# mLSTM gate rows stacked over 128 partitions in a two-layer hybrid trunk on one core

## The chip, the cores and the metric

The kernel runs on one core of one Trainium2 chip. What counts is its time on the device in microseconds (us), here the median of three runs. One further execution was recorded by the hardware profiler; all rows below are from that one.

## What is computed

Two layers of a block over 256 latent tokens with a prefix of 256 context tokens, width 1024. Each layer projects the normed tokens into the inputs of three branches (a bidirectional chunkwise mLSTM, grouped attention, a short convolution), merges them through gates, and ends with a squared-relu MLP. The change touches the mLSTM gates: an input gate i and a forget gate f for 2 directions and 4 heads, 16 numbers per token. Cut to that part:

```python
gates = (mg.reshape(bsz, n, 2, 2, M_HEADS) + gate_b).transpose(0, 2, 3, 4, 1)   # direction, i or f, head, token
for direction in range(2):
    rev = (lambda t: jnp.flip(t, axis=2)) if direction == 1 else (lambda t: t)
    ctx_state, h_c = run(q_c, k_c, v_c, g_c, init)        # log_i = g[:, direction, 0], log_f = log_sigmoid(g[:, direction, 1])
    _, h_l = run(q_l, k_l, v_l, g_l, ctx_state)
    outs.append((rev(h_l), rev(h_c)))
# in the scan, for each token t and each earlier token s:
#   w = exp(F_t - F_s + i_s - m_t),  F = running sum of log_f,  m = running maximum
#   h_t = sum_s (q_t . k_s) w v_s / max(|sum_s (q_t . k_s) w|, exp(-m_t))
```

The kernel does it for all 512 tokens at once, from rows per gate: F (running sum of log f), a = i - F, M (running maximum of a) and e = exp(-F - M).

## The kernel before

The tokens (512 columns: 256 context, 256 latent) stay transposed in SBUF, the model width over the partitions. All large products are done in a high and a low part (hH, hL, wH, wL), three products each, in panels of 256 output columns: SyncE loads a panel into raw, ScalarE writes its high part (L1428), VectorE the rest (L1845), TensorE runs the 48 products of it (run_panel). One list, PLAN, written by make_plan, sets the order of all steps, and each engine walks it in that order. Small steps lie between the panels. Four PSUM banks (pc) are shared by all small steps; `use(st, name, bank)` gives each step its bank and its turn on it, and TensorE claims a bank by waiting until the engine that read it before has freed it.

The steps that matter, in the order of PLAN, in each layer:

- gate_w: ScalarE and GpSimd write high and low part of the gate weights into wg, columns 0 to 15 and 32 to 47; the rest of wg is zero. GpSimd does its part after a few memsets, among them ones_row and M_parts.
- panels mk 0 and mk 1, then gate_tok (L1262, L1263): TensorE writes the gate rows to bank 1, 128 partitions of which 0 to 15 and 32 to 47 hold something. VectorE copies 48 partitions into g_rows and writes them reversed in time (context and latent each by itself) into g_back (L2103 to L2108).
- panel mq 0, then gate_sel (L1271, L1272): with the constant table sel, TensorE picks 8 rows (4 heads of either direction) for i into bank 2 and for f into bank 3, each from g_rows plus g_back: four products.
- gate_exp, gate_scan, gate_e, gate_e2 beside panels mq 1 and mv 0 to 2: VectorE and ScalarE make F_run, a_run, M_run, e_run (8 rows of 512 tokens) and their reversed forms a_back, M_back, e_back.
- gate_cols (L1280): TensorE turns the four row tiles a_run, a_back, e_run, e_back, each in four pieces of 128 tokens, so that tokens lie on partitions: 16 products with a corner of the identity. VectorE copies the 128 columns to g_col (L2156).
- weigh, weigh_late and value for each head. weigh spreads M over the partitions (m0, m1; L1293) and makes the scores of the first keys (s0, s1; L1300); weigh_late those of the last keys (s2; L1308). ScalarE and VectorE make the weights EP from them, GpSimd masks them (L1806), value (L1324) multiplies with v, into banks 0 to 3 in the order of its results, and VectorE evicts these (L2188 to L2199). In layer 1 only latent queries are computed: m0 and m1 share one bank, s0 and s1 another, and weigh, weigh_late follow value of the head before directly; then come norm_h, a panel mo, turn (banks 2 and 3; L1334) and the head's own value.

Of the kernel before, what the change touches and what calls it, by code (L numbers as in the profile page):

```python
# [20 lines left out]
F32 = mybir.dt.float32  # L21
F32R = mybir.dt.float32r
ALU = mybir.AluOpType
# [41 lines left out]
def make_constants():  # L65
# [32 lines left out]
    return np.concatenate([ident, row_sum, rot, np.cos(ang), np.sin(ang), sel.reshape(P, 32), one_row, pair_row],  # L98
# [6 lines left out]
CONST_COLS = FIRST_COLS + P + LAT + LAT + 32 + 8 + 8  # L105
# [76 lines left out]
def make_plan():  # L182
# [270 lines left out]
    for st in plan:  # L453
# [100 lines left out]
def trunk(nc, x, c, ctx_in, c_ctx, w_ada, b_ada, norm1, norm2, w_in, gate_b, mnorm, qnorm, knorm, conv_w,  # L554
          w_pm, w_pa, w_pc, w_out, w_up, w_down, fnorm, consts, out):
    ctx = ExitStack()
    with ctx:
# [18 lines left out]
        names = ["g_rows", "g_back", "f_pre", "f_neg", "f_exp", "log_f", "F_run", "a_run", "e_run"]  # L576
        rows = {n: at(n, [16, TOK], F32, Y + i * TOK * 4) for i, n in enumerate(names)}
        rows["a_back"] = at("a_back", [16, TOK], F32, Y + 9 * TOK * 4)
        rows["e_back"] = at("e_back", [16, TOK], F32, Y + 10 * TOK * 4)
# [5 lines left out]
        for n in ("g_rows", "g_back"):  # L585
            rows[n] = at(n + "_parts", [48, TOK], F32, Y + names.index(n) * TOK * 4)
# [26 lines left out]
        gb = at("gb", [8, 2], F32, T + 41600)  # L613
# [52 lines left out]
        sel = con[:, FIRST_COLS + P + 2 * LAT:CONST_COLS - 16].rearrange("p (g m) -> p g m", g=4)  # L666
# [71 lines left out]
        cols_in = sem("gate_cols_inputs")  # L738
        gc_ready = sem("gate_cols_ready")
# [178 lines left out]
        def _(sp):  # L918
# [48 lines left out]
            for st in PLAN:  # L967
                if st["k"] == "panel" and (st["kind"], st["c"]) == ("mk", 0):
# [7 lines left out]
                    for g in range(2):  # L976
                        for dr in range(2):
                            sp.dma_start(gb[dr * 4:dr * 4 + 4, g:g + 1],
                                         gate_b[l, dr, g].rearrange("(h a) -> h a", a=1)).then_inc(s_wg, 16)
# [24 lines left out]
        def _(pe):  # L1004
# [140 lines left out]
            for st in PLAN:  # L1145
# [119 lines left out]
                elif k == "gate_sel":  # L1265
# [153 lines left out]
        def _(act):  # L1419
# [25 lines left out]
            for st in PLAN:  # L1445
# [196 lines left out]
                elif k == "gate_e":  # L1642
# [5 lines left out]
                    act.activation(rows["e_run"][0:8, :], rows["e_run"][0:8, :], ACT.Exp).then_inc(eexp_ready, 1)  # L1648
# [72 lines left out]
        def _(pool):  # L1721
# [21 lines left out]
            for st in PLAN:  # L1743
# [22 lines left out]
                elif k == "apply":  # L1766
# [18 lines left out]
                    if st["n"] == 1 and j == NC - 1:  # L1785
# [3 lines left out]
                        pool.memset(rows["ones"][0:8, :], 1.0).then_inc(orow, 1)  # L1789
                        for t in M_parts:  # L1790
# [32 lines left out]
        def _(dve):  # L1823
# [25 lines left out]
            for st in PLAN:  # L1849
# [251 lines left out]
                elif k == "gate_tok":  # L2101
                    b = bank(dve, u["g"])
                    dve.tensor_copy(rows["g_rows"][:, :], b[0:48, :]).then_inc(gr_ready, 1)  # L2103
# [3 lines left out]
                    dve.tensor_copy(rows["g_back"][:, 0:CTX], rows["g_rows"][:, CTX - 1::-1]).then_inc(gr_ready, 1)  # L2107
                    dve.tensor_copy(rows["g_back"][:, CTX:TOK], rows["g_rows"][:, TOK - 1:CTX - 1:-1]).then_inc(gr_ready, 1)  # L2108
                elif k == "gate_sel":
# [4 lines left out]
                    b = bank(dve, u["f"])  # L2114
                    freed(dve.tensor_scalar(R["f_pre"], b[0:8, :], gb[0:8, 1:2], None, ALU.add), u["f"])
                    dve.wait_ge(free[u["f"][0]], u["f"][1] + 1)
                    dve.scalar_tensor_tensor(out=R["f_neg"], in0=R["f_pre"], scalar=-1.0, in1=R["f_pre"],
                                             op0=ALU.mult, op1=ALU.min).then_inc(fneg_ready, 1)
                elif k == "gate_scan":
# [7 lines left out]
                    b = bank(dve, u["i"])  # L2127
# [4 lines left out]
                    link(dve.tensor_tensor_scan(R["M_run"], R["a_run"], R["a_run"], 0.0, ALU.max, ALU.max))  # L2132
                    dve.scalar_tensor_tensor(out=R["e_run"], in0=R["F_run"], scalar=-1.0, in1=R["M_run"],
                                             op0=ALU.mult, op1=ALU.subtract).then_inc(erow_ready, 1)
                    for nm, fr in (("M_back", "M_run"), ("a_back", "a_run")):
                        start_link(dve.tensor_copy(R[nm][:, 0:CTX], R[fr][:, CTX - 1::-1]))
                        i = dve.tensor_copy(R[nm][:, CTX:TOK], R[fr][:, TOK - 1:CTX - 1:-1])
                        if nm == "M_back":
                            start_link(i)
                        else:  # L2140
                            i.then_inc(cols_in, 1)
# [230 lines left out]
```

## Time and profile before

| | before |
|---|---|
| median of 3 runs | 1871.84 us (1868.96 to 1871.91) |
| profiled execution, device time | 1873.62 us |
| its span, first to last instruction | 1871.9 us |
| TensorE (PE) busy | 1837.3 us, 98% |
| VectorE (DVE) busy | 1052.8 us, 56% |
| ScalarE (ACT) busy | 691.4 us, 37% |
| GpSimd (POOL) busy | 158.5 us, 8% |
| chain that ended last, share of PE | 92% |
| mean granted TensorE clock | 0.993 |

The busy time of an engine is the sum of its instructions, with matmuls that overlap counted once. A product appears as a weight load (PEld) and a matmul (PE); an fp32 product as two records of each. The shown duration of a matmul is longer than the distance to the next one, so distances of starts are what a product costs in a full queue.

### The profile page before, as it was taken

What the parts mean: (1) busy time and instruction counts of PE and PEld (TensorE: products, weight loads), DVE (VectorE), ACT (ScalarE), POOL (GpSimd) and SP (SyncE); (2) the same over time, 40 slices, a digit from 0 to 9 for tenths busy, and PEclk for the clock granted to TensorE, in tenths of its full rate; (3) what the DMA queues carried; (4) which work ended last, traced back from release to release, by engine and by line L of the source; (5) the groups of instructions that cost most, each with busy time, mean ns of one, the idle gap of its engine ahead of it and who ended that gap; (6) DMA issues with size and microseconds to landing.
All of it is one profiled execution on the core that took longest, in us unless ns stands there. A gap on an engine that the chain in (4) does not pass through costs nothing.

```text
span 1871.9 us, 24604 instructions
## 1 busy us (share of the span) xinstructions
PE 1837.3 (98%) x10087; PEld 1555.1 (83%) x10087; DVE 1052.8 (56%) x1535; ACT 691.4 (37%) x948; POOL 158.5 (8%) x158
## 2 busy tenths in 40 slices
PE   6999999999999999999999999999999999999998
PEld 4787788878888888878888888788898899999997
DVE  4534643554456675467675645644546656566555
ACT  3423543333222232234232323343534444445444
POOL 2101100000210011310000000300100110120000
PEclk9999999999999999999999999999999999999999
DMA  9221122112444444535444436232233265574563
GB/s 326 69 90 46 46 89 70 55 58 68 135 135 135 135 135 158 176 117 194 144 135 135 160 120 194 67 113 69 68 115 112 93 223 182 186 242 158 187 195 113
DMA packets 214271, 245.51 MB, mean 131 GB/s; under 512 B 5820, under 2 KB 186384, under 8 KB 214160
## 3 DMA queue, kind: packets, MB, share of 16 engines
q1 hardware_dynamic: 213856, 243.85, 40.2%
q8 instruction: 80, 1.31, 0.3%
q14 instruction: 31, 0.25, 0.0%
q10 hardware_dynamic: 304, 0.10, 0.0%
HBM read 242.88 MB, written 1.05 MB: 130 GB/s over the span
## 4 chain that ended last, share of the span: by engine, by line
PE 92%; DVE 3%; ACT 2%; SPq 1%; issue 1%; DMA 1%; POOL 0%; DVEq 0%; ACTq 0%
PE pp L1131 19%; PE pp L1135 18%; PE pp L1132 18%; PE pp L1138 4%; PE pp L1140 4%; PE pp L1139 4%; PE pc L1324 3%; PE pc L1376 2%; PE pp L1076 2%; PE pp L1077 2%; PE pp L1078 2%; PE pc L1036 2%; PE pc L1035 2%; PE pc L1037 2%; PE pc L1414 1%; SPq L934 1%
## 5 line engine op out<-in xcount | busy, mean ns | idle before, releaser
L1845 DVE TENSOR_TENSOR wL<-raw,wH 128x1024 fp32r<-128x1024 f32 x358 | 449.2, 1296 | 240.0 <-ACT wH L1428 237.2
L1131 PE MATMUL pp<-hH,wH 128*128 128x512 f32 (+1 forms) x1712 | 572.7, 345 | 0.7 <-ACT hH L1630 0.7
L1132 PE MATMUL pp<-hH,wL 128*128 128x512 f32 (+1 forms) x1712 | 562.8, 339 | 0.0
L1428 ACT ACTIVATE wH<-raw 128x1024 fp32r<-128x1024 f32 x360 | 360.3, 1049 | 303.2 <-PE pp L1140 106.8
L1135 PE MATMUL pp<-hL,wH 128*128 128x512 f32 (+1 forms) x1712 | 441.3, 339 | 1.4 <-POOL hL L1783 0.8
L1131 PEld LDWEIGHTS pp<-hH,wH 128*128 128x128 f32 x1712 | 325.1, 190 | 44.1 <-issue 9.1
L1132 PEld LDWEIGHTS pp<-hH,wL 128*128 128x128 f32 x1712 | 325.2, 190 | 36.2 <-issue 1.7
L1135 PEld LDWEIGHTS pp<-hL,wH 128*128 128x128 f32 x1712 | 295.4, 190 | 38.6 <-POOL hL L1783 2.5
L1131 PE MATMUL pp<-yH,wH 128*128 128x512 f32 (+1 forms) x320 | 115.3, 367 | 0.0
L1138 PE MATMUL pp<-yH,wH 128*128 128x512 f32 (+1 forms) x320 | 114.3, 357 | 0.0
L1140 PE MATMUL pp<-yH,wL 128*128 128x512 f32 (+1 forms) x320 | 114.3, 357 | 0.0
L1139 PE MATMUL pp<-yL,wH 128*128 128x512 f32 (+1 forms) x320 | 114.3, 357 | 0.0
L1132 PE MATMUL pp<-yH,wL 128*128 128x512 f32 (+1 forms) x320 | 112.3, 358 | 0.0
L2032 DVE SCALAR_TENSOR_TENSOR acc<-pair_W,c_wide,acc 128x512 f32<-128x512 f32 x126 | 102.2, 848 | 3.8 <-DVE xT L1980 1.2
L1135 PE MATMUL pp<-yL,wH 128*128 128x512 f32 (+1 forms) x320 | 88.3, 357 | 0.0
L1433 ACT ACTIVATE yH<-y_tmp 128x1024 fp32r<-128x1024 f32 (+1 forms) x48 | 40.6, 846 | 98.4 <-DVE y_tmp L1954 45.9
L1131 PEld LDWEIGHTS pp<-yH,wH 128*128 128x128 f32 x320 | 60.5, 189 | 11.0 <-issue 2.4
L1980 DVE SCALAR_TENSOR_TENSOR xT<-pp,modT,xT 128x256 f32<-128x256 f32 x88 | 36.7, 477 | 57.4 <-PE pp L1140 57.4
L1132 PEld LDWEIGHTS pp<-yH,wL 128*128 128x128 f32 x320 | 60.5, 189 | 9.3 <-issue 0.7
L1140 PEld LDWEIGHTS pp<-yH,wL 128*128 128x128 f32 x320 | 60.5, 189 | 8.8
L1138 PEld LDWEIGHTS pp<-yH,wH 128*128 128x128 f32 x320 | 60.5, 189 | 8.8
L1139 PEld LDWEIGHTS pp<-yL,wH 128*128 128x128 f32 x320 | 60.5, 189 | 8.7
(265 smaller groups left out, 2257.4 us busy)
## 6 DMA issues: line engine op xcount, KB each, us to landing
raw<-in_w_in SPq DMA_DIRECT2D x84, 1024.0 KB, 5.3
raw<-in_w_up SPq DMA_DIRECT2D x32, 1024.0 KB, 5.5
raw<-in_w_down SPq DMA_DIRECT2D x32, 1024.0 KB, 5.2
pair_W<-in_w_ada SPq DMA_DIRECT2D x10, 2048.0 KB, 7.9
ada_Y<-in_w_ada SPq DMA_DIRECT2D x10, 1024.0 KB, 12.5
ada_H<-in_w_ada SPq DMA_DIRECT2D x8, 1024.0 KB, 10.9
raw<-in_w_proj_m SPq DMA_DIRECT2D x8, 1024.0 KB, 5.1
raw<-in_w_proj_a SPq DMA_DIRECT2D x8, 1024.0 KB, 5.1
```

The lines of the kernel that those rows point to most:

```text
L1035: pe.matmul(banks[tt], yH[:, kt, ts_], wh[:, k_, :], start=first and k_ == 0, stop=False)
L1131: pe.matmul(dsts[b], wh[b], hi[:, kt, ts_], start=first, stop=False)
L1132: pe.matmul(dsts[b], wl[b], hi[:, kt, ts_], start=False, stop=False)
L1135: last = pe.matmul(dsts[b], wh[b], lo[:, kt, ts_], start=False, stop=end)
L1138: pe.matmul(dsts[b], wh[b], hi[:, kt, ts_], start=first, stop=False)
L1139: pe.matmul(dsts[b], wh[b], lo[:, kt, ts_], start=False, stop=False)
L1140: last = pe.matmul(dsts[b], wl[b], hi[:, kt, ts_], start=False, stop=end)
L1324: last = pe.matmul(b[:, 0:MV + 1], EP[:, d, off:off + P], vaug[:, s, h, :], start=i == 0, stop=i == len(terms) - 1)
L1428: act.activation(wH[:, p % HIGH, a:a + KH, :], raw[:, p % RAW, a:a + KH, :], ACT.Copy).then_inc(wH_ready, 1)
L1433: act.activation(yH[:, kts, ts_], src, ACT.Copy).then_inc(yH_ready, 1)
L1845: dve.tensor_tensor(wL[:, p % RAW, ks, :], raw[:, p % RAW, ks, :], wH[:, p % HIGH, ks, :].bitcast(F32), ALU.subtract).then_inc(wL_ready, 1)
L2032: i = dve.scalar_tensor_tensor(out=acc[:, v, :], in0=src[:, kt, :], scalar=c2[:, kt, v:v + 1], in1=acc[:, v, :], op0=ALU.mult, op1=ALU.add)
```

## The change

Three things. (1) The gate rows are kept in one tile g_both of 128 partitions, the forward rows on 0 to 63 and the reversed ones on 64 to 127, and the table sel becomes 128 x 40: one product gives i on partitions 0 to 7 and f on 32 to 39 of one bank, bank 2. The bank is freed after a_run was made; f's bias lies on partitions 32 to 39. (2) a_run, a_back, e_run and e_back become partitions 0, 32, 64 and 96 (8 each) of one tile, four, which GpSimd zeroes in full, after ones_row and ahead of M_parts; VectorE waits for that ahead of a_run. gate_cols turns it with four products, with the identity's first 8 columns of each group of 32 as the moving data, so the result is ordered by token piece first. (3) In layer 1 the banks of weigh for heads 1 to 3 are 0, 1, 2 for m0, s0, s2, not 1, 2, 3; head 0 keeps 1, 2, 3, and layer 0 its order.

```diff
-    sel = np.zeros((P, 4, 8), np.float32)
+    sel = np.zeros((P, 40), np.float32)
                 for part in (0, 32):
-                    sel[part + dr * 8 + g * 4 + h, g * 2 + dr, dr * 4 + h] = 1.0
+                    sel[64 * dr + part + dr * 8 + g * 4 + h, 32 * g + dr * 4 + h] = 1.0
...
-            use(st, "i", 2)
-            use(st, "f", 3)
+            use(st, "if", 2)
...
             for i, name in enumerate(("m0", "m1", "s0", "s1", "s2") if whole else ("m0", "s0", "s2")):
-                use(st, name, i % 4 if whole else i + 1)
+                use(st, name, i + 1 if st["h"] == 0 and not whole else i % 4)
...
+        g_both = at("g_both", [P, TOK], F32, Y)
+        four = at("four_rows", [P, TOK], F32, Y + TOK * 4)
...
-                    for name, g in (("i", 0), ("f", 1)):
-                        b = claim(u[name])
-                        pe.matmul(b[0:8, :], sel[0:48, 2 * g, :], rows["g_rows"][:, :], start=True, stop=False)
-                        last = pe.matmul(b[0:8, :], sel[0:48, 2 * g + 1, :], rows["g_back"][:, :], start=False, stop=True)
-                        filled(last, u[name])
+                    b = claim(u["if"])
+                    filled(pe.matmul(b[0:40, :], sel, g_both[:, :], start=True, stop=True), u["if"])
...
-                    for i, name in enumerate(("a_run", "a_back", "e_run", "e_back")):
-                        for tt in range(TT):
-                            c0 = (i * TT + tt) * 8
-                            last = pe.matmul(b[:, c0:c0 + 8], rows[name][0:8, tt * P:(tt + 1) * P], ident[0:8, 0:8],
-                                             start=True, stop=True)
+                    firsts = ident.rearrange("p (i n) -> p i n", i=4)[:, :, 0:8]
+                    for tt in range(TT):
+                        last = pe.matmul(b[:, tt * 32:(tt + 1) * 32], four[:, tt * P:(tt + 1) * P], firsts,
+                                         start=True, stop=True)
...
+                        pool.memset(four[:, :], 0.0).then_inc(four_zeroed, 1)
                         for t in M_parts:
...
-                    dve.tensor_copy(rows["g_rows"][:, :], b[0:48, :]).then_inc(gr_ready, 1)
+                    dve.tensor_copy(g_both[0:64, :], b[0:64, :]).then_inc(gr_ready, 1)
...
-                    dve.tensor_copy(rows["g_back"][:, 0:CTX], rows["g_rows"][:, CTX - 1::-1]).then_inc(gr_ready, 1)
+                    dve.tensor_copy(g_both[64:128, 0:CTX], g_both[0:64, CTX - 1::-1]).then_inc(gr_ready, 1)
...
-                    b = bank(dve, u["f"])
-                    freed(dve.tensor_scalar(R["f_pre"], b[0:8, :], gb[0:8, 1:2], None, ALU.add), u["f"])
+                    b = bank(dve, u["if"])
+                    link(dve.tensor_scalar(R["f_pre"], b[32:40, :], gb[32:40, 1:2], None, ALU.add))
...
+                    dve.wait_ge(four_zeroed, l + 1)
-                    dve.scalar_tensor_tensor(out=R["a_run"], in0=b[0:8, :], scalar=gb[0:8, 0:1], in1=R["F_run"],
+                    dve.scalar_tensor_tensor(out=four[0:8, :], in0=b[0:8, :], scalar=gb[0:8, 0:1], in1=R["F_run"],
                                              op0=ALU.add, op1=ALU.subtract).then_inc(cols_in, 1)
                     dve.wait_ge(cols_in, 4 * l + 1)
-                    dve.sem_inc(free[u["i"][0]], 1)
+                    dve.sem_inc(free[u["if"][0]], 1)
...
-                    dve.tensor_copy(g_col[:, :, :, :], b[:, 0:4 * TT * 8].rearrange("p (i t n) -> p i t n", i=4, t=TT)
+                    dve.tensor_copy(g_col[:, :, :, :], b[:, 0:4 * TT * 8].rearrange("p (t i n) -> p i t n", i=4, t=TT)
```

## Rows read from the trace of the kernel before

**Rows 1.** The page, busy times: us (share of the span) and instructions of PE
```profile
PE 1837.3 (98%) x10087; PEld 1555.1 (83%) x10087; DVE 1052.8 (56%) x1535; ACT 691.4 (37%) x948; POOL 158.5 (8%) x158
```

**Rows 2.** Waits of PE: engine line, waited for: us in total, times, longest
```profile
PE pc L1300 <- DVE hM L2196: 3.8, 3, 1.3
```

**Rows 3.** Timeline of PE, layer 0, selecting: start us, us, line, operands, count
```profile
65.67 0.39 PE L1131 MATMUL pp<-hH,wH 128*128 128x512 f32 x1
...
76.67 1.02 PE L1271 MATMUL pc<-g_rows_parts,con 48*8 48x512 f32 x2
...
80.31 0.79 PE L1131 MATMUL pp<-hH,wH 128*128 128x512 f32 x1
...
83.45 0.39 PE L1132 MATMUL pp<-hH,wL 128*128 128x512 f32 x1
```

**Rows 4.** Timeline of PE, layer 1, selecting products and what follows
```profile
1227.79 1.02 PE L1271 MATMUL pc<-g_rows_parts,con 48*8 48x512 f32 x2
1228.65 1.02 PE L1272 MATMUL pc<-g_back_parts,con 48*8 48x512 f32 x2
...
1231.32 0.39 PE L1131 MATMUL pp<-hH,wH 128*128 128x256 f32 x1
```

**Rows 5.** Timeline of PE, layer 0, turning products and what follows
```profile
125.51 1.05 PE L1280 MATMUL pc<-con,a_run 8*128 8x8 f32 x8
...
130.36 0.80 PE L1076 MATMUL pp<-wH,hH 128*128 128x512 f32 x1
...
134.73 0.40 PE L1077 MATMUL pp<-wL,hH 128*128 128x512 f32 x1
```

**Rows 6.** Timeline of PE, layer 1, turning products and what follows
```profile
1269.93 1.05 PE L1280 MATMUL pc<-con,a_run 8*128 8x8 f32 x8
...
1273.59 0.50 PE L1293 MATMUL pc<-M_parts,one_row 40*128 40x256 f32 x2
...
1278.19 0.39 PE L1076 MATMUL pp<-wH,hH 128*128 128x512 f32 x1
```

**Rows 7.** Windows: busy us (instructions) by engine, granted PE clock, DMA share, GB/s
```profile
80.00:81.00 1.00, 1.00 (x3) 0.59 (x3) 0.47 (x1) 0.00 (x0) 0.00 (x0) 0.51 1.02 395
...
1275.00:1276.00 1.00, 1.00 (x4) 0.82 (x3) 0.00 (x0) 1.00 (x5) 0.00 (x0) 0.50 0.00 0
1415.00:1416.00 1.00, 1.00 (x4) 0.48 (x3) 0.84 (x2) 0.00 (x0) 0.00 (x0) 0.50 1.09 389
```

**Rows 8.** Timeline of PE, layer 0, full small products of the attention
```profile
289.06 1.95 PE L1354 MATMUL pc<-con,small 128*128 128x128 f32 x16
290.85 1.84 PE L1344 MATMUL pc<-small,q_sq 128*128 128x1 f32 x16
```

**Rows 9.** Timeline of PE, layer 1, weigh of head 1, then its value
```profile
1300.31 0.50 PE L1293 MATMUL pc<-M_parts,one_row 40*128 40x256 f32 x2
1302.08 1.10 PE L1300 MATMUL pc<-qk 128*128 128x256 f32 x4 [1.28 <-DVE hM L2196]
1303.02 1.03 PE L1308 MATMUL pc<-qk 128*128 128x256 f32 x4
...
1304.00 0.28 PE L1132 MATMUL pp<-hH,wL 128*128 128x256 f32 x1
...
1310.07 1.25 PE L1324 MATMUL pc<-vaug,EP 128*128 128x257 f32 x5
```

**Rows 10.** Timelines of DVE and POOL, the same stretch
```profile
1301.45 0.48 DVE L2196 TENSOR_SCALAR hM<-pc,mstat 128x256 f32<-128x256 f32 x1
...
1306.52 1.13 POOL L1806 TENSOR_SCALAR_AFFINE_SELECT EP<-EP 128x128 f32<-128x128 f32 x4 [23.73 <-DVEq L2180]
```

**Rows 11.** Timelines of POOL and PE, layer 0, gate weights
```profile
30.72 0.96 POOL L1775 MEMSET wg<- 128x1024 f32 x1
...
56.58 1.45 POOL L1794 TENSOR_TENSOR wg<-w_gate,wg 128x128 fp32r<-128x128 f32 x1
...
61.94 0.40 PE L1262 MATMUL pc<-hH,wg 128*128 128x512 f32 x1
```

More of the change, by code:

```diff
@@ L104 @@
 C_WIDE = C_AT + 32
-CONST_COLS = FIRST_COLS + P + LAT + LAT + 32 + 8 + 8
+CONST_COLS = FIRST_COLS + P + LAT + LAT + 40 + 8 + 8
 def spans(l, d, s):
@@ L574, in trunk @@
         yL = at("yL", [P, KT, TOK], F32R, o); o += K16
[L576 to L579, printed above, removed]
+        names = ["f_pre", "f_neg", "f_exp", "log_f", "F_run"]
+        rows = {n: at(n, [16, TOK], F32, Y + (2 + i) * TOK * 4) for i, n in enumerate(names)}
+        g_both = at("g_both", [P, TOK], F32, Y)
+        four = at("four_rows", [P, TOK], F32, Y + TOK * 4)
         rows["ones"] = at("ones_row", [16, TOK], F32, Y + 11 * TOK * 4)
@@ L584, in trunk @@
         M_parts = [at(f"M_parts{i}", [40, TOK], F32R, Y + (14 + i) * TOK * 4) for i in range(2)]
-        for n in ("g_rows", "g_back"):
-            rows[n] = at(n + "_parts", [48, TOK], F32, Y + names.index(n) * TOK * 4)
         G = o
@@ L612, in trunk @@
         wg = at("wg", [P, KT, P], F32R, T + 26688)
-        gb = at("gb", [8, 2], F32, T + 41600)
+        gb = at("gb", [40, 2], F32, T + 41600)
         v_a = at("v_a", [P, TT, PC], F32, T)
@@ L738, in trunk @@
         cols_in = sem("gate_cols_inputs")
+        four_zeroed = sem("four_rows_zeroed")
         gc_ready = sem("gate_cols_ready")
@@ L1647, in _ @@
                         act.activation(M_parts[i][0:8, :], rows[n][0:8, :], ACT.Copy).then_inc(MH_ready, 1)
-                    act.activation(rows["e_run"][0:8, :], rows["e_run"][0:8, :], ACT.Exp).then_inc(eexp_ready, 1)
+                    act.activation(four[64:72, :], four[64:72, :], ACT.Exp).then_inc(eexp_ready, 1)
                 elif k == "weigh":
@@ L2102, in _ @@
                     b = bank(dve, u["g"])
-                    dve.tensor_copy(rows["g_rows"][:, :], b[0:48, :]).then_inc(gr_ready, 1)
+                    dve.tensor_copy(g_both[0:64, :], b[0:64, :]).then_inc(gr_ready, 1)
                     dve.wait_ge(gr_ready, 3 * l + 1)
                     dve.sem_inc(free[u["g"][0]], 1)
-                    dve.tensor_copy(rows["g_back"][:, 0:CTX], rows["g_rows"][:, CTX - 1::-1]).then_inc(gr_ready, 1)
-                    dve.tensor_copy(rows["g_back"][:, CTX:TOK], rows["g_rows"][:, TOK - 1:CTX - 1:-1]).then_inc(gr_ready, 1)
+                    dve.tensor_copy(g_both[64:128, 0:CTX], g_both[0:64, CTX - 1::-1]).then_inc(gr_ready, 1)
+                    dve.tensor_copy(g_both[64:128, CTX:TOK], g_both[0:64, TOK - 1:CTX - 1:-1]).then_inc(gr_ready, 1)
                 elif k == "gate_sel":
@@ L2126, in _ @@
                     link(dve.tensor_tensor_scan(R["F_run"], R["ones"], R["log_f"], 0.0, ALU.mult, ALU.add))
-                    b = bank(dve, u["i"])
-                    dve.scalar_tensor_tensor(out=R["a_run"], in0=b[0:8, :], scalar=gb[0:8, 0:1], in1=R["F_run"],
+                    b = bank(dve, u["if"])
+                    dve.wait_ge(four_zeroed, l + 1)
+                    dve.scalar_tensor_tensor(out=four[0:8, :], in0=b[0:8, :], scalar=gb[0:8, 0:1], in1=R["F_run"],
                                              op0=ALU.add, op1=ALU.subtract).then_inc(cols_in, 1)
                     dve.wait_ge(cols_in, 4 * l + 1)
-                    dve.sem_inc(free[u["i"][0]], 1)
-                    link(dve.tensor_tensor_scan(R["M_run"], R["a_run"], R["a_run"], 0.0, ALU.max, ALU.max))
-                    dve.scalar_tensor_tensor(out=R["e_run"], in0=R["F_run"], scalar=-1.0, in1=R["M_run"],
+                    dve.sem_inc(free[u["if"][0]], 1)
+                    link(dve.tensor_tensor_scan(R["M_run"], four[0:8, :], four[0:8, :], 0.0, ALU.max, ALU.max))
+                    dve.scalar_tensor_tensor(out=four[64:72, :], in0=R["F_run"], scalar=-1.0, in1=R["M_run"],
                                              op0=ALU.mult, op1=ALU.subtract).then_inc(erow_ready, 1)
[L2135 to L2141, printed above, removed]
+                    start_link(dve.tensor_copy(R["M_back"][:, 0:CTX], R["M_run"][:, CTX - 1::-1]))
+                    start_link(dve.tensor_copy(R["M_back"][:, CTX:TOK], R["M_run"][:, TOK - 1:CTX - 1:-1]))
+                    start_link(dve.tensor_copy(four[32:40, 0:CTX], four[0:8, CTX - 1::-1]))
+                    dve.tensor_copy(four[32:40, CTX:TOK], four[0:8, TOK - 1:CTX - 1:-1]).then_inc(cols_in, 1)
                     dve.wait_ge(dchain, count[0])
@@ L2151, in _ @@
                     dve.wait_ge(eexp_ready, l + 1)
-                    dve.tensor_copy(R["e_back"][:, 0:CTX], R["e_run"][:, CTX - 1::-1]).then_inc(cols_in, 1)
-                    dve.tensor_copy(R["e_back"][:, CTX:TOK], R["e_run"][:, TOK - 1:CTX - 1:-1]).then_inc(cols_in, 1)
+                    dve.tensor_copy(four[96:104, 0:CTX], four[64:72, CTX - 1::-1]).then_inc(cols_in, 1)
+                    dve.tensor_copy(four[96:104, CTX:TOK], four[64:72, TOK - 1:CTX - 1:-1]).then_inc(cols_in, 1)
                 elif k == "gate_cols":
                     b = bank(dve, u["g"])
-                    dve.tensor_copy(g_col[:, :, :, :], b[:, 0:4 * TT * 8].rearrange("p (i t n) -> p i t n", i=4, t=TT)
+                    dve.tensor_copy(g_col[:, :, :, :], b[:, 0:4 * TT * 8].rearrange("p (t i n) -> p i t n", i=4, t=TT)
                                     ).then_inc(gc_ready, 1)
```

7 lines of the change are left out of this document (3 added, 4 removed).

## The prediction

> **What bounds the kernel now.** I read the page's busy shares and clock line first, then TensorE's waits, then its timeline around the gate steps, then the granted clock in one-microsecond windows. TensorE (PE) is busy 1837.3 us of the 1871.9 us span, 98% [rows 1]. So the kernel is a stream of products in one queue: whatever takes a product out of that queue shortens the run by the product's time, and whatever VectorE or ScalarE do beside it costs nothing until they are late. In the list of PE's waits one line belongs to this change: the score products of L1300 waited for the h_out evictions of L2196 three times, 3.8 us in all [rows 2]. No line of that list names a weight panel. The windows show a third thing that the busy share hides: after the gate steps PE is still busy the whole microsecond, but at a granted clock of 0.50 to 0.51, that is 1.2 in place of 2.4 GHz [rows 7].
>
> **The change part by part.** All starts are PE's. A step's cost is the time from its first start to the first start of what follows, because each product's shown duration overlaps the next one.
>
> The selecting products (step gate_sel, L1271 and L1272). Four fp32 products of 512 columns, two records each, become one. In layer 1 the first pair starts at 1227.79 and the next at 1228.65: 0.86 us a product; all four last from 1227.79 to 1231.32, 3.53 us with the changeovers [rows 4]. The new product has 128 rows and 40 columns of weights, not 48 by 8. Below: 0.86 us, if only the streamed columns count. Above: in head 1 two full 128x128 products of 256 columns last from 1302.08 to 1303.02, 0.94 us [rows 9], so twice one of them, 0.94 us, for 512 columns. I take 0.86, since the streamed columns are the same 512. That saves 3 x 0.86 = 2.58 us a layer, 5.16 us in both (5.0 at the upper price).
>
> The turning products (step gate_cols, L1280). Sixteen 8-row products with 8 columns become four 128-row ones with 32 columns. In layer 1 sixteen last from 1269.93 to 1273.59, 3.66 us, or 0.227 us each once one short changeover is taken off [rows 6]. Sixteen records, eight products, of full 128x128 weights and 128 columns last from 289.06 to 290.85, so 0.224 us each [rows 8]: between 8 and 128 rows, and 8 and 128 columns, the price does not move, and 32 columns lie between. Nothing here shows moving data in four groups of eight columns; below I set it at no extra cost, above at twice the price, 0.22 us more for each, 1.8 us in all, and I take the lower, as the price is the weights' and not the columns'. Saved: 12 x 0.227 = 2.72 us a layer, 5.44 us in both (3.6 at the upper price).
>
> The clock. After the selecting products of layer 0 seven products of 512 columns take from 80.31 to 83.45, 3.14 us [rows 3], where such a product at full clock takes 0.2275 (the panel before the gate step, 48 products from 65.67 to 76.67, less a changeover of 0.09), so 1.59 us: 1.55 lost, and 3.64 against 3.53 us for the four selecting products themselves, together 1.66 us [rows 3, 4]. In layer 0's turning step: 125.51 to 130.36 is 4.85 us against 3.66, and the ten products after it, 130.36 to 134.73, 4.37 against 2.28: 1.19 + 2.09 = 3.28 us lost [rows 5, 6]. In layer 1, 1273.59 to 1278.19 is 4.60 us; the same work at full clock is 0.50 for L1293, 0.94 and 0.86 for the two pairs of scores (in head 1: 1302.08 to 1303.02, and 1303.02 to 1304.00 less one small product of 0.12), and three times 0.2275: 2.98 us, so 1.62 lost [rows 6, 9]. Sum 6.56 us. Each of the three stretches begins after more than 2 us of these tiny products back to back, and PE did not stand idle ahead of them; the same four selecting products in layer 1 were followed by no slow stretch, so what is issued sets how likely a fall is, and where it happens to lie decides. After the change only 0.9 us of such work stands together in each place, and eight full-array products of 1.79 us were followed by none [rows 8]. So I expect all three falls to go. Bounds: none of it comes back, 0; all of it, 6.56. I take all of it for the profiled execution. A fourth fall, in layer 1's attention, is not touched [rows 7].
> The page "TensorE: Matmul & The Clock Gate" of the Trainium skill (Part 1: The HAM clock gate) says that the engine drops to half clock after it has stood idle, and advises against idle gaps. By that rule a change that takes away no idle time gives back no clock; the windows disagree, with PE busy 1.00 of 1.00 us in the slow microseconds and no idle in the rows before them [rows 3, 5, 7].
>
> The banks of heads 1 to 3 in layer 1 (step weigh). Now m0, s0, s2 lie in banks 1, 2, 3, right after the value step, whose four results lie in banks 0 to 3 and are evicted in that order. m0 starts at 1300.31, and s0 must wait until bank 2 is emptied by the L2196 eviction that starts at 1301.45 and lasts 0.48 us: it starts at 1302.08 after 1.28 us of idling [rows 9, 10]. With banks 0, 1, 2, m0 and s0 find theirs emptied by the pair of evictions before; s0 runs inside the idle time, for 0.94 us, and s2 meets the same eviction at 1302.08. What is left of the stall is 1.28 - 0.94 = 0.34 us. Saved: 0.94 us a head, 2.82 us. Bounds: 0 if the next wait closes in, 3.8 if all stall went. What is late next: value of head 1 starts at 1310.07 and needs the masked weights; the mask on GpSimd starts at 1306.52 and lasts 1.13 us, to 1307.65 [rows 9, 10]. Its inputs hang on ScalarE and on the value step's last result, not on s0, so it stays; PE would come at 1309.13, 1.5 us later. That holds. The turn step (banks 2 and 3) and the next value step claim banks that were free for longer than that.
>
> Edits at nothing. GpSimd zeroes one more tile of 128x512 ahead of the low half of the gate weights. Nearest row: 128x1024 in 0.96 us, so some 0.5. Below 0, above 0.96. In layer 0 the low half ends at 58.03 and PE reads it at 61.94: 3.9 us of cover [rows 11]. VectorE's new wait on that memset stands ahead of a_run, with the panel splits queued behind it, but the memset is done some 30 us before. Copies of 64 partitions in place of 48, reversed into partitions 64 to 127, and bias DMAs to partitions 32 and up (as many as before) are the same instructions with the same columns, off PE's path. Bank 2 is held from gate_sel to gate_scan; no step on PE claims it or bank 3 in between. The constants grow by 8 columns of a load that PE doesn't wait for.
>
> **The sum.** The profiled execution took 1873.62 us, 1.7 more than its span. 5.16 + 5.44 + 2.82 + 6.56 = 19.98, so 1853.6 us. The median of the runs before, 1871.84, is 1.8 us shorter, about one slow stretch of 1.6; the runs spread over 2.9. So the median has about one stretch less to give back: 13.42 + 4.8 = 18.2, which gives 1853.6 again. Forecast 1853.6 us.
>
> **The rivals.**
> (B) The clock doesn't come back: the falls stay or move to other clusters of small products. For it: the fall was absent once with the same work, and everything later now lies elsewhere. Against: the small clusters shrink to 0.9 us. Time: 1871.84 - 13.42 = 1858.4. The Trainium skill's idle rule, cited above, would give this time. Chance 0.22.
> (C) The banks give nothing, because the stall moves whole to s2 or to value. Against it: the 1.5 us worked out above. Time: 1853.6 + 2.8 = 1856.4. Chance 0.08.
> (D) Slower: the memset on GpSimd delays the gate weights. It costs nothing up to 3.9 us and all above that; to end slower it would have to last some 15 us in each layer, against 0.96 for twice the columns. A time then of 1876 or more. Chance 0.03.
> (E) The gain is given back to the feeding of panels: PE arrives sooner at each panel than its load and its splits. Against: PE's waits name no panel, and loads are issued when a panel is done, so they move along. If it took nearly all, 1870. Chance 0.05.
>
> **How the numbers follow.** The forecast has 0.62, with its own range 1850.5 to 1857 (prices of the new products +2, clock -2 to +3, run to run 1.5). The range to 8 in 10 takes in (B) and (C): 1849 to 1859. A measurement of this kernel can tell about 0.2%, 3.7 us, from no change: forecast, (B) and (C) lie beyond it, 0.92 faster; (E) is within, 0.05; (D) 0.03 slower.
>
> **What would show it.** In the profile after: one selecting product of two records and about 0.86 us; four turning products of about 0.9 us in all; at the first products after both a granted clock of 1.00, in both layers; L1300's wait gone from the list and the one on L1308 at about 0.3 us, three times. Wrong would be: turning products of over 0.3 us each, slow stretches of some 3 us in the gate steps or new ones elsewhere, a wait ahead of value or gate_tok, or a new line of PE waiting for panels.

## The result and the profile after

The changed kernel takes 1851.74 us, median of 4 runs (1851.62 to 1851.84), against 1870.4 us for the kernel before in the same comparison: a ratio of 0.990, 95% interval 0.9883 to 0.9918. The forecast was 1853.6 us with 1849 to 1859 around it. The profiled execution took 1851.64 us, its span was 1849.9 us, so 22.0 us less than the profiled execution before.

The page of the kernel after, busy times; it answers to [rows 1]:

```profile
PE 1819.1 (98%) x10027; PEld 1543.8 (83%) x10027; DVE 1052.4 (57%) x1535; ACT 691.4 (37%) x948; POOL 157.9 (9%) x160
```

PE's busy time fell by 18.2 us and its share stays 98%. The kernel is still one queue of products, only shorter.

Waits of PE after, the longest (line, waited for: us in total, times, longest); it answers to [rows 2]:

```profile
PE pc L1184 <- DVE n_sum L2059: 5.3, 3, 4.2
```

This is a wait at a norm, 5.3 us before too, and waits at the start of the kernel come next, as before. The 3.8 us on the score products (L1300 before, L1294 after) are gone from the list.

Timeline of PE in layer 0, the selecting product, what follows, and then the turning products, what follows and the eleventh panel product; it answers to [rows 3, 5]:

```profile
76.59 1.05 PE L1268 MATMUL pc<-g_both,con 128*40 128x512 f32 x2
77.58 0.50 PE L1129 MATMUL pp<-hH,wH 128*128 128x512 f32 x1
...
121.24 0.97 PE L1274 MATMUL pc<-con,four_rows 128*128 128x32 f32 x8
122.04 0.48 PE L1074 MATMUL pp<-wH,hH 128*128 128x512 f32 x1
...
124.44 0.39 PE L1075 MATMUL pp<-wL,hH 128*128 128x512 f32 x1
```

The selecting step lasts 0.99 us, not 3.64, and the turning step 0.80 us, not 4.85. The ten panel products after the turning step take 2.40 us (122.04 to 124.44), where they took 4.37.

The same in layer 1; it answers to [rows 4, 6]:

```profile
1217.38 1.05 PE L1268 MATMUL pc<-g_both,con 128*40 128x512 f32 x2
1218.36 0.38 PE L1129 MATMUL pp<-hH,wH 128*128 128x256 f32 x1
...
1256.88 0.97 PE L1274 MATMUL pc<-con,four_rows 128*128 128x32 f32 x8
1257.78 0.50 PE L1287 MATMUL pc<-M_parts,one_row 40*128 40x256 f32 x2
...
1260.74 0.40 PE L1074 MATMUL pp<-wH,hH 128*128 128x512 f32 x1
```

Here they last 0.98 us (3.53 before) and 0.90 us (3.66 before), and from the spreading product L1287 to the fourth panel product 2.96 us, where it was 4.60.

Windows of the kernel after (busy us of each engine, granted clock, DMA share, GB/s); they answer to [rows 7]:

```profile
80.00:81.00 1.00, 1.00 (x6) 0.84 (x5) 0.00 (x0) 1.00 (x1) 0.00 (x0) 1.00 1.02 397
122.00:123.00 1.00, 1.00 (x6) 0.87 (x6) 0.61 (x2) 1.00 (x2) 0.00 (x0) 1.00 0.34 39
1258.00:1260.00 2.00, 2.00 (x11) 1.69 (x10) 0.18 (x1) 1.62 (x5) 0.00 (x0) 1.00 0.91 232
1394.00:1397.00 3.00, 2.89 (x12) 1.86 (x13) 2.52 (x5) 1.28 (x1) 0.00 (x0) 1.00 0.76 269
```

The granted clock is 1.00 after each gate step, and also in the attention of layer 1 (the last row), where it was 0.50 before. In this whole profile it is 0.50 only within the first 29 us and behind PE's last product, from 1847.8 on.

Timeline of PE in layer 1, weigh of head 1 and its value, then VectorE's eviction that frees bank 2; they answer to [rows 9, 10]:

```profile
1282.86 0.50 PE L1287 MATMUL pc<-M_parts,one_row 40*128 40x256 f32 x2
1283.28 1.13 PE L1294 MATMUL pc<-qk 128*128 128x256 f32 x4
1284.54 1.13 PE L1302 MATMUL pc<-qk 128*128 128x256 f32 x4
...
1291.69 0.60 PE L1318 MATMUL pc<-vaug,EP 128*128 128x257 f32 x2
```

```profile
1284.00 0.48 DVE L2188 TENSOR_SCALAR hM<-pc,mstat 128x256 f32<-128x256 f32 x1
```

s0 (L1294) now follows the spreading product at once. s2 (L1302) starts 1.26 us after s0, 0.94 of which are s0's own work by [rows 9]: a stall of 0.32 us is left, and it ends as the eviction that starts at 1284.00 does. The distance of head 1's value from that of head 2 is 14.99 us (15.92 before).

The two profiles can be laid side by side at steps that both have; the lead of the kernel after at each is what had been won by then:

| PE starts | before | after | lead, us | won in this stretch | forecast |
|---|---|---|---|---|---|
| selecting products, layer 0 | 76.67 | 76.59 | 0.08 | | |
| turning products, layer 0 | 125.51 | 121.24 | 4.27 | 4.19 | 2.58 + 1.66 |
| eleventh panel product after them | 134.73 | 124.44 | 10.29 | 6.02 | 2.72 + 3.28 |
| turning products, layer 1 | 1269.93 | 1256.88 | 13.05 | 2.76 | 2.58 |
| fourth panel product after them | 1278.19 | 1260.74 | 17.45 | 4.40 | 2.72 + 1.62 |
| value of head 3, layer 1 | 1341.91 | 1321.68 | 20.23 | 2.78 | 2.82 |
| L1366 (L1360 after), behind scores in the attention, layer 1 | 1418.26 | 1396.32 | 21.94 | 1.71 | 0 |

Nothing was lost on the way and nothing given back; the last row is a gain that the sum did not have.

### The profile page after: what moved, and what is told of

It is laid out like the page before. It is cut to its first block, busy times and chain, and to the rows that moved or that the text cites. A ratio compares the mean times of both kernels' runs of the same rounds, so it can differ in the third digit from the quotient of the medians.

```text
span 1849.9 us, 24486 instructions
## 1 busy us (share of the span) xinstructions
PE 1819.1 (98%) x10027; PEld 1543.8 (83%) x10027; DVE 1052.4 (57%) x1535; ACT 691.4 (37%) x948; POOL 157.9 (9%) x160
## 4 chain that ended last, share of the span: by engine, by line
PE 93%; DVE 2%; ACT 2%; SPq 1%; DMA 1%; issue 1%; POOL 0%; DVEq 0%; ACTq 0%
PE pp L1129 19%; PE pp L1133 19%; PE pp L1130 19%; PE pp L1136 4%; PE pp L1138 4%; PE pp L1137 4%; PE pc L1318 3%; PE pc L1370 2%; PE pp L1074 2%; PE pp L1075 2%; PE pp L1076 2%; PE pc L1035 2%; PE pc L1034 2%; PE pc L1033 2%; PE pc L1408 1%; SPq L932 1%
```

## Experiments

One number is needed to read the times. In the comparisons the kernel before ran 25 times on one chip, and its times are no smooth spread but a ladder: 1867.2, 1868.9, 1870.5, 1872.1 and 1873.7 us, rungs 1.6 apart. Each profile can be put on it by counting its slow stretches, the places in which the granted clock is 0.50 for 3.4 us (the 6.8 us stretch in layer 0 counts twice). Left out of the count are the stretch behind PE's last product and the one in the first 30 us: the latter lasts 3.4 us in one profile, 6.8 in most and 10.2 in two, and the selecting step of layer 0 starts within 0.4 us of the same time in all of them. One such stretch costs (1873.7 - 1867.2) / 4 = 1.63 us.

**The kernel before once more.** No edit.

> The kernel before, once more, for the spread of its own runs and a second look at where the clock falls. Theory A (small products bring the clock down, and where they happen to lie decides): times between 1868 and 1874 us that differ by multiples of about 1.6 us, mean granted clocks that go with them, and in this profile slow stretches of about 3 us only after clusters of small products (gate_sel, gate_cols, weigh, the attention of layer 1), not all at the same places as in the first profile. Rival B (the clock falls at fixed places): the same four places, and a spread that the mean clock does not follow.

Median 1872.05 us (1867.2 to 1873.8, 11 runs). Windows of its profile:

```profile
81.00:82.00 1.00, 1.00 (x3) 0.75 (x3) 0.95 (x2) 0.00 (x0) 0.00 (x0) 0.50 0.21 78
129.00:130.00 1.00, 1.00 (x6) 1.00 (x6) 0.00 (x0) 0.00 (x0) 0.00 (x0) 0.50 1.08 384
1276.00:1277.00 1.00, 1.00 (x3) 0.79 (x3) 0.00 (x0) 1.00 (x5) 0.00 (x0) 0.50 0.00 0
1416.00:1417.00 1.00, 1.00 (x2) 0.34 (x1) 0.38 (x1) 0.34 (x1) 0.00 (x0) 0.50 0.50 165
```

The mean clock of a run sets only the lowest rungs apart: 0.997 for the one run at 1867.2 us, 0.994 for the ten others, from 1870.4 to 1873.8. The profiled execution, 1873.65 us, has stretches at the same four places as the first one (five by count), so one half of theory A's expectation failed: it was to show them at other places. But a kernel whose times take five values cannot have the same stretches each time, and the kernels with one part below show them at fewer places.

**Only the selecting product.**

```diff
-            use(st, "i", 2)
-            use(st, "f", 3)
+            use(st, "if", 2)
...
+                    b = claim(u["if"])
+                    filled(pe.matmul(b[0:40, :], sel, g_both[:, :], start=True, stop=True), u["if"])
```

> Only the selecting product: four become one, the turning products and the banks stay as before. By the sum: 2 x 2.58 = 5.2 us less work on TensorE, and the fall after gate_sel in layer 0 (1.66 us) goes: 1863.5 to 1865 us against a before of 1870.4. Theory A: no granted clock under 0.97 in the 4 us after gate_sel in either layer, the falls after gate_cols stay. Rival B (the falls do not come from these products): 5.2 us only, about 1865, and the layer 0 stretch is still slow.

1866.68 us (1865.0 to 1866.9, 9 runs), ratio 0.9973 (0.9963 to 0.9982). Windows after gate_sel in layer 0, after gate_cols in layer 0, after gate_cols in layer 1:

```profile
80.00:83.00 3.00, 3.00 (x15) 2.49 (x14) 0.00 (x0) 2.97 (x4) 0.00 (x0) 1.00 0.49 189
125.00:128.00 3.00, 3.00 (x11) 2.69 (x11) 1.50 (x3) 0.00 (x0) 0.00 (x0) 0.50 0.45 157
1268.00:1270.00 2.00, 2.00 (x6) 1.59 (x5) 0.00 (x0) 2.00 (x7) 0.00 (x0) 0.50 0.03 10
```

Full clock after gate_sel, 0.50 after both turning steps, as theory A had it. The median is above the expected range of 1863.5 to 1865: four runs lie at 1865.0 to 1865.5, where the three stretches of this profile put them, and five lie at 1866.7 to 1866.9, about one stretch higher. Where those have it was not profiled.

**Only the turning products.**

```diff
-                    for i, name in enumerate(("a_run", "a_back", "e_run", "e_back")):
...
+                    firsts = ident.rearrange("p (i n) -> p i n", i=4)[:, :, 0:8]
+                    for tt in range(TT):
+                        last = pe.matmul(b[:, tt * 32:(tt + 1) * 32], four[:, tt * P:(tt + 1) * P], firsts,
...
+                        pool.memset(four[:, :], 0.0).then_inc(four_zeroed, 1)
```

> Only the turning products: sixteen become four, the selecting products and the banks stay as before. By the sum: 2 x 2.72 = 5.4 us less work, and 3.3 + 1.6 us of slow clock after gate_cols go: about 1860.5 against 1870.4. Theory A: full clock after gate_cols in both layers, the fall after gate_sel in layer 0 may stay. Rival B: 5.4 us only, about 1865.

1861.42 us (1859.6 to 1863.2, 5 runs), ratio 0.9948 (0.9933 to 0.9963). The same places:

```profile
80.00:83.00 3.00, 3.00 (x7) 2.13 (x7) 1.42 (x2) 0.89 (x2) 0.00 (x0) 0.52 0.41 157
125.00:128.00 3.00, 3.00 (x18) 2.58 (x18) 1.35 (x2) 2.01 (x2) 0.00 (x0) 1.00 0.34 79
1265.00:1268.00 3.00, 3.00 (x15) 2.56 (x14) 0.03 (x1) 2.77 (x9) 0.00 (x0) 1.00 1.00 308
```

The other way round: 0.52 after the four 48x8 products, 1.00 after the turning steps. For the turning steps the two runs tie the slow stretches to their cluster. For the selecting step they do not by themselves: two of the five runs here, at 1859.6 and 1859.8 us, lie where a run without any slow stretch would (table below), although both layers still have the four 48x8 products.

**Only the banks.**

```diff
-                use(st, name, i % 4 if whole else i + 1)
+                use(st, name, i + 1 if st["h"] == 0 and not whole else i % 4)
```

> Only the banks of heads 1 to 3 in layer 1. By the sum: each of three stalls of 1.28 us shrinks to 0.34, 2.8 us in all: 1867.6 against 1870.4, with the distance from one head's value step to the next 0.94 us shorter (15.92 to 14.98 us). Rival C (the next wait closes in): under 1 us, 1869.5 or more.

1869.05 us (1865.9 to 1870.8, 11 runs), ratio 0.999 (0.9981 to 0.9998). Timeline of PE, value of head 0, the scores s0 of head 1, and its value:

```profile
1290.93 6.23 PE L1324 MATMUL pc<-vaug,EP 128*128 128x257 f32 x28
...
1297.52 1.13 PE L1300 MATMUL pc<-qk 128*128 128x256 f32 x4
...
1305.93 1.25 PE L1324 MATMUL pc<-vaug,EP 128*128 128x257 f32 x5
```

s0 starts 6.59 us after the value step's first product (7.93 before, from 1294.15 to 1302.08), and the values are 15.0 us apart (15.92 before). The median alone, 1.5 us better, would have said little: the ladder of this kernel is 1865.9, 1867.6, 1869.1, 1870.8, and the four upper rungs of before moved down by 2.8 us give 1866.1, 1867.7, 1869.3, 1870.9. The saving is as expected; how many stretches come along varies.

This profile shows one thing more. The four 48x8 selecting products of layer 0 are unchanged here (76.63 to 80.16), and no slow stretch follows them:

```profile
80.00:83.00 3.00, 3.00 (x13) 2.36 (x13) 1.42 (x2) 1.13 (x2) 0.00 (x0) 1.00 0.35 135
```

So in the four profiles that have four 48x8 products, they were followed by a fall in layer 0 of three (both profiles of before, and the turning products alone) and in layer 1 of none: three of eight steps. A single selecting product was followed by none in twelve steps of six profiles. That fits the selecting products as the cause of their fall, but it is far from the sixteen turning products, which were followed by one in each of the ten steps profiled.

Taking the stretches out of each profiled execution leaves what is work and waiting:

| kernel | profiled, us | slow stretches | less 1.63 each | against before |
|---|---|---|---|---|
| before | 1873.65 | 5 | 1865.5 | |
| only the selecting product | 1865.45 | 3 | 1860.6 | 4.9 |
| only the turning products | 1862.94 | 2 | 1859.7 | 5.8 |
| only the banks | 1865.93 | 2 | 1862.7 | 2.8 |
| all three | 1851.64 | 0 | 1851.6 | 13.9 |

The parts add up, 13.5 to 13.9, and the forecast had 13.4. This difference of profiles rests on the count and on 1.63 us for each stretch.

**The changed kernel once more.** No edit.

> The changed kernel once more. The kernel before has a ladder of times, 1867.2, 1868.9, 1870.5, 1872.1 and 1873.7, one rung for each slow stretch of 1.6 us. Theory A: the changed kernel has lost the clusters of the gate steps, so nearly all of its runs sit on the lowest rung, 1851.7, and only the attention of layer 1, which the change does not touch, can lift some to 1853.3. Rival B (its four runs so far were on one rung by luck): runs spread over three or more rungs, up to 1856.6.

1851.8, 1852.0, 1852.0 and 1853.4 us: theory A. Of eight runs of this kernel seven lie on the lowest rung and one on the next.

**Four selecting products, 128 rows by 40 columns.**

```diff
-                    filled(pe.matmul(b[0:40, :], sel, g_both[:, :], start=True, stop=True), u["if"])
+                    for i in range(4):
+                        last = pe.matmul(b[0:40, :], sel, g_both[:, :], start=True, stop=True)
+                    filled(last, u["if"])
```

> The changed kernel with its one selecting product (128 rows, 40 columns of weights, 512 columns streamed) issued four times, only the last one counting. Three more products of 0.86 us a layer: 5.2 us more, 1856.9 without a slow stretch. Theory A1 (the clock falls when little of the array is in use, and 128x40 is still little): slow stretches after gate_sel come back in some runs, 1856.9 to 1860. Theory A2 (it fell only for the tiny 48x8 and 8x8 operands): 1856.9 and full clock in both layers.

1856.9, 1857.1, 1858.4 and 1858.9 us. Timeline of PE in layer 0:

```profile
76.94 3.63 PE L1269 MATMUL pc<-g_both,con 128*40 128x512 f32 x8
80.50 0.50 PE L1129 MATMUL pp<-hH,wH 128*128 128x512 f32 x1
80.84 0.40 PE L1130 MATMUL pp<-hH,wL 128*128 128x512 f32 x1
81.07 0.39 PE L1129 MATMUL pp<-hH,wH 128*128 128x512 f32 x1
```

Four products last 3.56 us, 0.86 each and one changeover, so three cost what was forecast to be saved. The panel products that follow are 0.23 us apart: full clock, in layer 1 too. The profiled execution (1858.87 us) has its one slow stretch from 1399.6 on, in the attention. This fits theory A2, but does not decide for it: four 48x8 products too were followed by no fall in five of eight steps, and where the run at 1858.4 us had its stretch was not profiled.

**Three full products and the selecting one.**

```diff
+                    for i in range(3):
+                        pe.matmul(b[:, :], ident, g_both[:, :], start=True, stop=True)
                     filled(pe.matmul(b[0:40, :], sel, g_both[:, :], start=True, stop=True), u["if"])
```

> The same four products, but three of them with the full 128x128 identity as weights, before the selecting one; their result is overwritten. Theories A1 and A2: the full array counts as work, no slow stretch, 1856.9 to 1857.3 us. Rival (any fp32 cluster of over 3 us brings the clock down, whatever it fills): slow stretches after gate_sel as in the run with four 40-column products.

Three runs at 1857.0 to 1857.1 and one at 1858.9 us, no slow stretch in the profile. So the rival's fall came in neither layer: 3.65 us of fp32 products by themselves needn't bring the clock down. The step takes 3.65 us against 3.56: one changeover more, between the two kinds of weights, as the identity's products stand 0.86 us apart too (two records of 0.43). Here again it is two steps of one profile.

**Sixteen turning products of 128 rows.**

```diff
-                    for tt in range(TT):
+                    for tt in [tt for tt in range(TT) for _ in range(4)]:
```

> The changed kernel with each of the four turning products issued four times: sixteen products as before, but of 128 rows and 32 columns. Twelve more of 0.225 us a layer: 5.4 us more, 1857.1 without a slow stretch. Price theory: the cost hangs on their number, so gate_cols takes 3.6 us again in both layers at full clock. Theory A1: what brings the clock down is many short products that stream few columns, so slow stretches after gate_cols come back in both layers, up to 1862. Theory A2: 128 rows in use keep the clock up, 1857.1.

1858.9, 1860.5, 1860.6 and 1863.8 us. Timeline of PE in layer 0, then windows in both layers:

```profile
121.47 3.65 PE L1274 MATMUL pc<-con,four_rows 128*128 128x32 f32 x32
124.96 0.48 PE L1074 MATMUL pp<-wH,hH 128*128 128x512 f32 x1
...
128.59 0.49 PE L1074 MATMUL pp<-wH,hH 128*128 128x512 f32 x1
```

```profile
125.00:128.00 3.00, 3.00 (x10) 2.39 (x10) 2.65 (x3) 0.00 (x0) 0.00 (x0) 0.56 0.44 152
1265.00:1268.00 3.00, 3.00 (x9) 2.42 (x9) 0.29 (x1) 2.42 (x8) 0.00 (x0) 0.57 0.39 135
```

Sixteen products last 3.49 us, 0.22 each with 128 rows and 32 columns, against 0.227 with 8 rows and 8 columns: between these sizes the price hangs on their number. And the clock falls behind them again, in both layers. The nine panel products from 124.96 to 128.59 take 3.63 us and not 2.05. So for the turning step the rows in use don't keep the clock up; what is left is that sixteen short products stand in a row, by their number or by the time they take. Theory A1 here; for the selecting step theory A2 is not refuted.

**Rows or columns.** The old selecting product had 48 rows and 8 columns. Two kernels put four more products ahead of the selecting one:

```diff
+                    for i in range(4):
+                        pe.matmul(b[0:8, :], sel[:, 0:8], g_both[:, :], start=True, stop=True)
```

> The changed kernel with four more fp32 products of 512 columns ahead of the selecting one in each layer, all overwritten: 128 rows and 8 columns of weights. Eight times 0.86 us more: 1858.7 without a slow stretch. Four of 48x8 were followed by a slow stretch in layer 0 in every profile that had them, four of 128x40 by none. Theory R (rows in use decide): full clock after gate_sel, 1858.7. Theory C (columns in use decide): a slow stretch after gate_sel of layer 0 at least, 1860.3 or 1862.

```diff
+                    for i in range(4):
+                        pe.matmul(b[0:40, :], sel[0:48, :], g_both[0:48, :], start=True, stop=True)
```

> The same with 48 rows and 40 columns of weights: 1858.7 without a slow stretch. Theory R (rows decide): a slow stretch after gate_sel of layer 0 at least, 1860.3 or 1862. Theory C (columns decide): full clock after it, 1858.7. If both kernels show slow stretches, it is rows times columns; if neither does, it is something else about the old products, their order in two banks for one.

Both have two of four runs on 1858.7 to 1859.1 us and two on 1860.4 to 1860.7. Timeline of PE in layer 1, first with 128x8 (profiled execution 1858.87 us), then with 48x40 (1860.55 us):

```profile
1224.60 1.05 PE L1270 MATMUL pc<-g_both,con 128*40 128x512 f32 x2
1225.58 0.39 PE L1129 MATMUL pp<-hH,wH 128*128 128x256 f32 x1
1225.81 0.28 PE L1130 MATMUL pp<-hH,wL 128*128 128x256 f32 x1
1225.92 0.29 PE L1129 MATMUL pp<-hH,wH 128*128 128x256 f32 x1
```

```profile
1224.87 1.93 PE L1270 MATMUL pc<-g_both,con 128*40 128x512 f32 x2
1226.73 0.58 PE L1129 MATMUL pp<-hH,wH 128*128 128x256 f32 x1
1227.11 0.41 PE L1130 MATMUL pp<-hH,wL 128*128 128x256 f32 x1
1227.33 0.41 PE L1129 MATMUL pp<-hH,wH 128*128 128x256 f32 x1
```

With 128 rows the profile has no slow stretch. With 48 rows the clock falls inside the step, at 1224.6, in the fourth of the added products: the selecting product takes 1.86 us and not 0.98, the panel products after it 0.22 and not 0.12. It does so in layer 1 and not in layer 0. That speaks for the rows, weakly. Over all profiles four or more products with 48 rows were followed by or had a fall in four of ten steps, those with 128 rows in none of six; at four in ten, six clear steps in a row still come up about once in twenty. The other kernel's two upper runs were not profiled either, so which of its steps brought their stretch is open. The expectation for this run also starts from a sentence that the profiles contradict: after four 48x8 products layer 0 had a slow stretch in three profiles of four, not in every one. What I had expected, a stretch in layer 0 for one of the two, came for neither.

**weigh_late behind a quarter of the panel.** The stall that is left, filled with other work:

```diff
-            if more:
+            if more or h:
                 part("mo", l, h, 0, 0, 2)
```

> The changed kernel with weigh_late of heads 1 to 3 in layer 1 moved behind the first quarter of the panel mo, as layer 0 has it, so that the 0.34 us that it still stalls for bank 2 has other work in it. Three times 0.34: 1.0 us less, 1850.8 against 1851.8. Rival: the weights of head h come later for it, or the turn step waits for bank 2, and nothing is won or up to 0.5 us lost.

1850.4, 1852.2, 1852.3 and 1852.3 us, a median of 1852.26. Timeline of PE, value of head 0 to value of head 1 (profiled execution 1850.43 us):

```profile
1276.64 6.23 PE L1318 MATMUL pc<-vaug,EP 128*128 128x257 f32 x28
...
1285.62 1.03 PE L1302 MATMUL pc<-qk 128*128 128x256 f32 x4
...
1291.24 6.23 PE L1318 MATMUL pc<-vaug,EP 128*128 128x257 f32 x28
```

The values are 14.60 us apart, not 14.99. So 1.2 us went in three heads, and the median is no better. A second look:

> The same kernel as in the run late, once more. There the distance from value to value fell from 14.99 to 14.61 us, 1.2 us in three heads, and the lowest time was 1850.4 against 1851.6, but three of four runs lay 1.8 us above it. Theory A: those three had a slow stretch more, after the attention of layer 1 as its small products lie 1.2 us earlier; the runs lie on 1850.4 and 1852.3 only, and which rung is the commoner one cannot be told beforehand. Rival B: the reordering itself costs in most executions, and the profile of a run on the upper rung shows full clock and a longer step elsewhere.

1852.2 to 1852.5 us, all four on the upper rung. Window of its profile (1852.37 us) in the attention of layer 1:

```profile
1394.00:1395.00 1.00, 1.00 (x3) 0.48 (x2) 0.69 (x1) 0.00 (x0) 0.00 (x0) 0.50 1.09 387
```

The clock falls at 1393.4, in the attention, and the execution is 1.9 us longer than the profiled one above: theory A. Of all its runs seven of eight lie one stretch up (the place was profiled in one); of the changed kernel's eight one does. So what PE won by the reordering went to a slow stretch in a step that was not edited, which now starts 1.2 us earlier. That the shift is the cause is not shown: the chips differed too (8 and 7 here, 2 for the changed kernel's second four runs). The two profiles of this one kernel, each over 4.00 us up to the same point of the attention (in the second the fall), first without and then with it:

```profile
1389.16:1393.16 4.00, 2.82 (x26) 2.59 (x25) 3.49 (x7) 2.14 (x3) 0.00 (x0) 1.00 0.37 92
1389.44:1393.44 4.00, 2.82 (x26) 2.59 (x25) 3.50 (x7) 2.15 (x3) 0.00 (x0) 1.00 0.38 95
```

PE's busy time there is the same, 2.82 of 4.00 us, and yet the clock falls in only one: the work ahead of that point does not decide alone. The reordering does not beat the changed kernel.

## Why the prediction was right

**What bounds it.** Right. PE is the queue, and each product taken out shortened the run by its distance to the next. No panel was waited for, so rival (E) fell: the lead only grows down the table of starts.

**The selecting products.** 5.16 us forecast. The profile has 0.99 and 0.98 us for the new step: the product of 0.86 and a changeover, as in [rows 4]. The kernel with four shows 0.86 for a product of 128x40, the lower bound (128x128 weights took the same). Taken from the starts, 3.53 - 0.98 = 2.55 us in layer 1.

**The turning products.** 5.44 us forecast with the new product at 0.224 us. Four last 0.80 and 0.90 us, 0.20 to 0.225 each; four groups of eight moving columns cost nothing extra. The upper bound of twice the price is out.

**The clock.** 6.56 us forecast, and all three stretches are gone. For the turning steps, 4.90 us of it, the cause is shown: sixteen short products were followed by a fall in all ten profiled steps, four in none of eighteen. For the selecting step, 1.66 us, it is likely and no more, with three falls in eight steps before and none in twelve after. Taking all of it in was right for the execution that was profiled, whose count of five was the highest seen; a run of before at 1867.2 us had one stretch to give back. The work of layer 1 behind the turning step, 2.98 us at full clock by my sum, takes 2.96; its first term, 0.50 for L1293, was the shown duration, where the distance of starts is 0.43 (1273.59 to 1274.02), and the scores make up for it.

Rival (B), at 1858.4 us, lies 6.7 us above the measured time. The rule of the Trainium skill ("TensorE: Matmul & The Clock Gate", Part 1) that the clock falls after idling would have given that time. The traces contradict it in one place and leave it in another. Behind the sixteen turning products the clock falls with PE busy 1.00 of 1.00 us. In the attention of layer 1 PE was busy 2.82 of the 4.00 us before the fall (the windows of the last kernel above), so idling may have its part there, but the same idling was also followed by no fall.

**The banks.** 2.82 us forecast, 2.78 measured. The stall left is 0.32 us for 0.34. I had said where it would be seen, on L1308 in the list of waits: there it is not. It shows only as the distance of two starts. Value was not late: rival (C) is out.

**The memset.** Timeline of GpSimd in layer 0, the new memset and the low half of the gate weights:

```profile
55.53 0.52 POOL L1784 MEMSET four_rows<- 128x512 f32 x1
...
56.96 0.79 POOL L1789 TENSOR_TENSOR wg<-w_gate,wg 128x128 fp32r<-128x128 f32 x1
```

0.52 us for an estimate of 0.5. The gate weights are ready by 57.8, against 61.9 when PE reads them. Rival (D) is out.

**The sum.** The term that was mis-sized is the last one, the attention's stretch, set at nothing. I left it in, as the change does not touch that step; it went, for 1.71 us. That step's own code is unchanged and lies 20 us earlier; that this is the cause is argued, not shown. The fall there also comes and goes without the whole change: it is in both profiles of before and with the turning products alone, and missing with the selecting product alone and with the banks alone. And I took the median of before, 1871.84 us of three runs, to be one stretch below the profiled one. That holds for those three; the 25 runs have a median of 1870.57 us, three stretches, not four. So the time after came out 1.9 us under the forecast, about the one stretch left in, while the gain against the wider median is 18.8 us for a forecast 18.2. That the gain fits so well is partly luck: the median had one stretch less to lose than I took, and the attention's came on top.

## What to carry to other kernels

Where TensorE is the bound, count small fp32 products one by one: rows and columns of the weights hardly move their price (0.22 us from 8x8 to 128x128 when few columns are streamed, 0.86 at 512, from 48x8 to 128x128), so stack them over partitions and over columns until they are few. Then look at the granted clock behind each cluster of them, because the panels after it can pay as much again. Count falls over several executions and at every step that has the cluster; one profile with a fall and one without show little. And a stall of a product on a PSUM bank is also cured by the order in which banks are handed out: give the next step's first results the banks that are evicted first.

## What the runs showed of the hardware

- The clock of a fully busy TensorE falls from 2.4 to 1.2 GHz (granted 1.00 to 0.50) behind sixteen short fp32 products (3.5 us, 8x8 or 128x32), in ten of ten profiled steps, though the runs at 1867.2 us, with one stretch by count, must have had at least one turning step without. Four short ones (0.8 us) were followed by a fall in none of the nine profiles that have them. Behind four long ones with 48x8 weights (3.5 us) it fell in three of eight steps, and behind four or five long ones with 128 rows in none of six, which is too few to part the two. Each fall costs 1.63 us, and whether one comes at a given place varies from execution to execution.
- The times of such a kernel form a ladder. A small gain can't be read from medians of a few runs that lie on different rungs: 2.8 us of work saved showed as 1.5, and 1.2 us saved as 0.5 lost (medians of eight runs each, 1851.8 and 1852.3). Comparing rung with rung, or the starts of the same step in two profiles, reads them to 0.1 us.
- A fall does not stay with the code that it hits. The attention of layer 1 had a stretch in both profiles of before, in at most one of eight runs with everything ahead of it 20 us shorter, and, by the times and one profile, in seven of eight with that 1.2 us shorter still. That the shift does it is not shown.
- Left open: whether the rows, or the rows times the columns, in use keep the clock up for long products at all, and what in the short ones brings it down at 128 rows.
